# Four moved query units, a decoding laid out by ranks, and four PSUM banks for the token rows of a two-layer diffusion block

## The reference

```python
q = (xc @ wq).reshape(128, 8, 2, 128)                 # 8 heads, two half queries
s1 = einsum('thd,hnd->thn', q[:, :, 0], k1)           # scores against 128 keys, twice
s2 = einsum('thd,hnd->thn', q[:, :, 1], k2)
v1, i1 = top_k(s1, 16);  v2, i2 = top_k(s2, 16)
cand = v1[..., :, None] + v2[..., None, :]            # 16 x 16 pairs
cidx = i1[..., :, None] * 128 + i2[..., None, :]
top_s, pos = top_k(cand, 16)
eidx = take_along_axis(cidx, pos)                     # 16 experts for each head: 128 per token
g = softmax(top_s)
h = gelu(einsum('thkd,td->thk', eu[eidx], xc))        # a dot with each expert's row
y = einsum('thk,thkd->td', g * h, ev[eidx])           # weighted sum of its other row
```

## Time and profile before

| | |
|---|---|
| three runs | 2995.09, 3000.06, 3001.91 us; median 3000.06 |
| profiled execution | 2992.15 us, of which the span is 2990.3 |
| busy | PE 2379.1 us (80%), DVE 1900.5 (64%), ACT 469.3 (16%), POOL 729.8 (24%) |
| TensorE's granted clock | 0.798 of full speed on average |
| DMA | 1029.87 MB, mean 344 GB/s; the gathers are 805.36 MB of it |

### The profile page before, as it was taken

One profiled execution on the slowest core, in us unless ns is written; L12 is line 12 of the kernel. 1 busy time (PEld: TensorE's weight loads), 2 busy tenths in 40 slices (PEclk: granted clock), 3 DMA queues, 4 the chain that ended last, 5 costly groups with the idle time before them and its releaser, 6 DMA issues.

```text
span 2990.3 us, 34802 instructions
## 1 busy us (share of the span) xinstructions
PE 2379.1 (80%) x11960; PEld 1309.5 (44%) x11960; DVE 1900.5 (64%) x6178; ACT 469.3 (16%) x1139; POOL 729.8 (24%) x779
## 2 busy tenths in 40 slices
PE   7989997878999778567979988887798576665565
PEld 6868893444656445124545543332695111121111
DVE  2879987776655557857854455665458855555555
ACT  3151131233010011012010012221321010000000
POOL 0000003222222222332223223332002333333332
PEclk7999997887999889568979987675898556566557
DMA  8718858998999989879999999999445989999997
GB/s 309 273 61 318 312 213 328 388 375 332 406 384 414 414 320 369 343 319 370 373 377 420 420 403 384 404 397 373 177 148 231 367 348 418 400 381 418 402 400 287
DMA packets 155376, 1029.87 MB, mean 344 GB/s; under 512 B 19136, under 2 KB 29888, under 8 KB 34496
## 3 DMA queue, kind: packets, MB, share of 16 engines
q0 software_dynamic: 110592, 805.36, 66.8%
q1 hardware_dynamic: 31648, 209.70, 18.0%
q10 hardware_dynamic: 12960, 12.59, 1.3%
HBM read 1018.66 MB, written 8.91 MB: 344 GB/s over the span
## 4 chain that ended last, share of the span: by engine, by line
PE 52%; DVE 21%; DMA 19%; issue 3%; ACT 3%; POOL 1%; ACTq 1%; DVEq 0%; SPq 0%; POOLq 0%
DMA ring<-in_peer_uv,eT 17%; PE PS L1434 14%; DVE ring L2625 9%; PE PS L972 8%; PE PS L1453 6%; PE PS L894 4%; PE PS L999 2%; PE PS L1018 2%; PE PS L1084 2%; PE PS L896 1%; POOL ring L784 1%; PE PS L1287 1%; PE PS L1188 1%; PE PS L1061 1%; PE PS L851 1%
## 5 line engine op out<-in xcount | busy, mean ns | idle before, releaser
L2625 DVE CUSTOM_DVE_ANT_0 ring<-ring,PS 128x512 f32<-128x512 f32 x1536 | 994.1, 684 | 772.4 <-PE PS L1453 598.0
L784 POOL DMA_INDIRECT ring<-in_peer_uv,eT x768 | 728.2, 948 | 2230.1 <-PE PS L1434 1397.1
L1453 PE MATMUL PS<-xr,onesb 3*128 3x512 bf16 x1536 | 517.7, 470 | 396.3 <-DVE hcol L2625 335.8
L1434 PE MATMUL PS<-ring,zcol 128*32 128x512 f32 x3072 | 566.4, 876 | 90.1 <-DVE zcol L2635 88.3
L1453 PEld LDWEIGHTS PS<-xr,onesb 3*128 3x128 bf16 x1536 | 105.1, 95 | 920.3 <-DVE hcol L2625 496.9
L1434 PEld LDWEIGHTS PS<-ring,zcol 128*32 128x32 f32 x3072 | 102.0, 140 | 368.8 <-issue 219.6
L972 PE MATMUL PS<-uT,W 128*128 128x256 f32 x1024 | 246.4, 389 | 0.0
L1937 ACT ACTIVATE ge<-hdot 128x4 f32<-128x4 f32 x192 | 39.5, 206 | 1281.0 <-DVE hdot L2630 1281.0
L972 PEld LDWEIGHTS PS<-uT,W 128*128 128x128 f32 x1024 | 191.6, 192 | 48.2 <-issue 23.4
L2012 DVE CUSTOM_DVE_ANT_0 ring<-ring 128x1024 f32<-128x1024 f32 x160 | 190.1, 1221 | 8.1 <-DMA ring<-in_w_rows 3.9
L894 PE MATMUL PS<-uT,W 128*128 128x256 f32 (+1 forms) x672 | 154.5, 383 | 8.2 <-ACT uT L1526 7.8
(11 more groups left out here) (358 smaller groups left out, 2313.9 us busy)
## 6 DMA issues: line engine op xcount, KB each, us to landing
ring<-in_w_rows SPq DMA_DIRECT2D x40, 1024.0 KB, 8.1
W<-in_w_in SPq DMA_DIRECT2D x30, 1024.0 KB, 9.4
W<-in_w_gate SPq DMA_DIRECT2D x16, 1408.0 KB, 6.2
W<-in_w_gate SPq DMA_DIRECT2D x16, 1280.0 KB, 7.5
W<-in_w_out SPq DMA_DIRECT2D x20, 1024.0 KB, 5.0
W<-in_w_gate SPq DMA_DIRECT2D x16, 1152.0 KB, 10.5
ring<-in_w_q SPq DMA_DIRECT2D x16, 1024.0 KB, 13.5
xr<-xrows ACTq DMA_DIRECT2D x768, 6.0 KB
```

The costliest lines, as they stand in the source:

```text
L784: pool.indirect_dma_start(ring[:, slot, :], None, (peer_uv0, peer_uv1)[b.l], bass.IndirectOffsetOnAxis(eT[:, f % 2, t:t + 1], 0)).then_inc ...
L1434: last = T.matmul(PS[k * NR:(k + 1) * NR, (6 + h) * 512:(7 + h) * 512], zcol[:, g % 2, k, NR - 1 - at:2 * NR - 1 - at], ring[:, slot, D + ...
L1453: T.matmul(bank(x_bank(q, n) + h), onesb[p0:p0 + 3, 0:1].to_broadcast([3, P]), xr[p0:p0 + 3, g % 2, h * 512:(h + 1) * 512], start=True, st ...
L2625: V.tensor_tensor_reduce(out=u_half, in0=u_half, in1=bank(x_bank(q, n) + h), scale=1.0, scalar=0.0, op0=ALU.mult, op1=ALU.add, accum_out=h ...
```

## The change

1. In a latent block's end the last four query units of the second tile (`BEHIND = 4`), with the scores that need them, are formed in the first "late" steps, behind `TILE_READY`, where tokens run. The indices are turned behind unit 8 and the weights behind unit 9; the token rows are asked for behind unit 5.
2. `picked` lays its table out as place, rank, head, with the eight heads innermost, always for all heads. The reduction becomes four sums of halves. `decoded` writes the ranks with heads innermost, and `places_kept` lays out the kept indices so.
3. In the stages named in `X_BANKS` the token rows of LAT0 and CTX0 have four PSUM banks (0, 1, 4, 5), and TensorE sends the next token's broadcast along with a token's own where both fall into the same stage (`x_ahead`). The units of all fronts and the output products of the context back have two banks (2 and 3) instead of four. `x_back` waits for the dots that read a bank before a stage uses it otherwise.
4. Small constants share a tile; `iota_b` holds each number eight times.

```diff
+BEHIND = 4
+X_BANKS = {("front", "unit"): (0, 1, 4, 5), ("front", "sel"): (0, 1, 4, 5),
+           ("back", "out"): (0, 1, 4, 5)}
...
-        def x_bank(q, n):
-
-            return 2 * (n % 2) if ORDER[q] == LAT1 and n >= P else 0
+        def x_plan(stages):
+
+            banks, used = [], {}
+            for n in range(len(ORDER) * TOK):
+                own = X_BANKS.get(stages[n], (0, 1)) if n < 2 * TOK else (2, 3) if n >= 2 * TOK + P and n % 2 else (0, 1)
+                for h in range(2):
+                    b = min(own, key=lambda k: used.get(k, -1)) if len(own) > 2 else own[h]
+                    used[b] = len(banks)
+                    banks.append(b)
+            return banks
+
+        def x_ahead(stages, n):
+
+            return len(X_BANKS.get(stages[n], (0, 1))) - 2 if n + 1 < 2 * TOK and stages[n] == stages[n + 1] else 0
...
+        def unit_bank(n, c1=TOK):
+
+            return bank(2 + n % 2, 0, c1)
...
-                    if n >= 4:
-                        evacuated(n - 4)
+                    if n >= 2:
+                        evacuated(n - 2)
...
-                for u in range(16):
+                for u in range(16 - BEHIND):
                     unit(1, u)
...
-                    if u == 11:
+                    if u == 8:
                         pe.wait_ge(a["xcut"], a.at("xcut", 3))
                         pe.wait_ge(a["idx"], a.at("idx", 1))
                         T.transpose(bank(6, 0, P), isel_a[:, 0, :], ident[:, :]).then_inc(a["idxT"], 1)
-                    if u == 13:
+                    if u == 9:
                         pe.wait_ge(a["sel"], a.at("sel", 1))
                         T.transpose(bank(7, 0, P), ts[:, :, :].rearrange("p h k -> p (h k)"), ident[:, :]).then_inc(a["selT"], 1)
-                scores(1, 7)
-                pe.wait_ge(a["wo_s"], a.at("wo_s", base + 32))
                 yield TILE_READY
                 for q in range(LATE):
+                    u = 16 - BEHIND + q
+                    if u < 16:
+                        unit(1, u)
+                    if u <= 16 and u % 2 == 0:
+                        scores(1, u // 2 - 1)
                     yield "late"
...
                 r0, r1, r2 = row_banks(f, tt)
+                x_back(2, 3, 4, 5)
...
+            def x_back(*banks):
+
+                for b in banks:
+                    if x_used.get(b, -1) >= 0:
+                        pe.wait_ge(dotted, x_used[b] + 1)
+
+            def broadcast(i):
+                whole, h = i // 2, i % 2
+                q, g, k = whole // TOK, whole % TOK // GRP, whole % GRP
+                if k == 0 and h == 0:
+                    pe.wait_ge(xr_land[g % 2], 16 * (q * NG // 2 + g // 2 + 1) * GRP)
+                x_back(x_banks[i])
+                x_used[x_banks[i]] = i
+                p0 = 32 * ((k + h) % GRP)
+                T.matmul(bank(x_banks[i]), onesb[p0:p0 + 3, 0:1].to_broadcast([3, P]),
+                         xr[p0:p0 + 3, g % 2, h * 512:(h + 1) * 512], start=True, stop=True).then_inc(xb_s, 1)
...
+                        while sent[0] < 2 * whole + 2 + x_ahead(woven["pool"].stages, whole):
+                            broadcast(sent[0])
+                            sent[0] += 1
...
-                for h0 in (0, HEADS // 2):
-                    for e in range(2):
-                        picked(1, h0, HEADS // 2, e, hot_s, isel_s)
-                        yield
+                for e in range(2):
+                    picked(1, e, hot_s, isel_s)
+                    yield
...
+            def places_kept(tt):
+
+                ch.link(V.tensor_copy(i16f[:, tt, :, :, :],
+                                      i16[:, tt * SEG:(tt + 1) * SEG, :].rearrange("p (h e) k -> p e k h", e=2)))
+
+            def picked(tt, e, hot, index):
+
+                grid = [P, TOPK, TOPK, HEADS]
+                ch.link(V.tensor_tensor(hot[:, :, :, :], abf[:, e, :].rearrange("p (k h) -> p k h", h=HEADS).unsqueeze(1).to_broadcast(grid),
+                                        iota_b[:, :, :].unsqueeze(2).to_broadcast(grid), ALU.is_equal))
+                ch.link(V.tensor_tensor(hot[:, :, :, :], hot[:, :, :, :], i16f[:, tt, e, :, :].unsqueeze(2).to_broadcast(grid), ALU.mult))
+                for width in (8, 4, 2):
+                    ch.link(V.tensor_tensor(hot[:, 0:width, :, :], hot[:, 0:width, :, :], hot[:, width:2 * width, :, :], ALU.add))
+                ch.link(V.tensor_tensor(index[:, e, :].rearrange("p (h k) -> p k h", h=HEADS), hot[:, 0, :, :], hot[:, 1, :, :], ALU.add))
```

More of the change, by code:

```diff
@@ L138, in __init__ @@
         self.seen, self.ready, self.done, self.limit = [], 0, 0, TT * P
+        self.stage, self.stages = None, []
     def token(self, experts):
+        self.stages.append(self.stage)
         next(experts)
@@ L154, in run @@
                 self.seen.append(step)
+                self.stage = (what, step)
                 if step == TILE_READY:
@@ L166, in run @@
                 self.limit += P
+            self.stage = None
 class Chain:
@@ L278, in build @@
         band = sb("band", [P, TT, TOK])
-        iota_b = sb("iota_b", [P, TOPK], BF16)
-        iota = sb("iota", [P, TOPK])
-        ones = sb("ones", [P, 1])
+        iota_b = sb("iota_b", [P, TOPK, HEADS], BF16)
+        hsum = sb("hsum", [P, 2, HEADS])
+        iota = hsum[:, :, :].rearrange("p a h -> p (a h)")
+        singles = sb("singles", [P, 4])
+        ones, zero, eps = [singles[:, k:k + 1] for k in range(3)]
         onesb = sb("onesb", [P, 1], BF16)
@@ L1208, in back @@
                 begun = []
+                if s == 1:
+                    x_back(4, 5)
                 if b.early:
@@ L1244, in back @@
                         slot = arrived()
-                    if n >= 4:
-                        pe.wait_ge(a["wo_s"], a.at("wo_s", n - 3))
+                    if n >= 2:
+                        pe.wait_ge(a["wo_s"], a.at("wo_s", n - 1))
                     for k in range(KD):
-                        last = T.matmul(bank(2 + n % 4, 0, TOK), W[:, slot, k * 2 * P + n % 2 * P:k * 2 * P + (n % 2 + 1) * P],
+                        last = T.matmul(unit_bank(n), W[:, slot, k * 2 * P + n % 2 * P:k * 2 * P + (n % 2 + 1) * P],
                                         mT[:, k, :], start=(k == 0), stop=(k == KD - 1))
@@ L1444, in experts @@
                             pe.wait_ge(a["sel_s"], a.at("sel_s", 2))
-                        if k == 0:
-                            pe.wait_ge(xr_land[g % 2], 16 * (q * NG // 2 + g // 2 + 1) * GRP)
-                        for h in range(2):
-                            if whole:
-                                turns = 1 if n and x_bank(q, n) != x_bank(q, n - 1) else 0
-                                if whole > turns:
-                                    pe.wait_ge(dotted, 2 * (whole - turns) - 1 + h)
-                            p0 = 32 * ((k + h) % GRP)
-                            T.matmul(bank(x_bank(q, n) + h), onesb[p0:p0 + 3, 0:1].to_broadcast([3, P]),
-                                     xr[p0:p0 + 3, g % 2, h * 512:(h + 1) * 512], start=True, stop=True)\
-                                .then_inc(xb_s, 1)
+                        while sent[0] < 2 * whole + 2 + x_ahead(woven["pool"].stages, whole):
+                            broadcast(sent[0])
+                            sent[0] += 1
                         if k == 0 and g % NR:
@@ L1566, in front @@
                 if r in BESIDE:
-                    chosen(BESIDE[r], at_of["back", BESIDE[r]], 1, 5)
+                    chosen(BESIDE[r], at_of["back", BESIDE[r]], 1, 3)
                     yield "sel"
@@ L1721, in apart @@
                         x_rows(b.f, 1)
+                    if u == 7:
+                        exponents(a, 0)
                     if u == 8:
-                        exponents(a, 0)
-                    if u == 11:
                         act.wait_ge(a["idxT"], a.at("idxT", 1))
                         A(eT[:, b.f % 2, 0:P], bank(6, 0, P), ACT.Copy).then_inc(a["sel_s"], 1)
-                    if u == 13:
+                    if u == 9:
                         act.wait_ge(a["selT"], a.at("selT", 1))
                         A(gT[:, b.f % 2, 0:P], bank(7, 0, P), ACT.Copy).then_inc(a["sel_s"], 1)
-                scores(1, 7)
                 yield TILE_READY
                 for q in range(LATE):
+                    u = 16 - BEHIND + q
+                    if u < 16:
+                        unit(1, u)
+                    if u <= 16 and u % 2 == 0:
+                        scores(1, u // 2 - 1)
                     yield "late"
@@ L2507, in apart @@
                 bounded_pairs(a)
-                ch.link(V.tensor_copy(i16f[:, 0:SEG, :], i16[:, 0:SEG, :]))
-                decoded(0, HEADS, dec_a)
-                for h0 in (0, HEADS // 2):
-                    for e in range(2):
-                        picked(0, h0, HEADS // 2, e, hot_a, isel_a)
+                places_kept(0)
+                decoded(dec_a)
+                for e in range(2):
```

(2 more changed lines are left out.)

87 lines of the change are left out of this document (41 added, 46 removed).

## The result

Seven runs of the changed kernel gave 2977.18 to 2988.87 us, median 2983.32; seven of the kernel before 2995.09 to 3002.0, median 2996.45. The ratio is 0.9946 (0.9933 to 0.9958), some 16 us; it is worked out from all the runs, and the two medians alone lie 13 us apart. Forecast were 2980 against 3000, a ratio of 0.9933, 20 us.

What follows compares the result with a forecast made beforehand. DMA transfers were taken as 90 to 100% busy in nearly every window from the first gather on. Starts 10, late gathers -2, selections 6 and fronts 6 make 20 us off the median 3000.06: 2980 us, range 2962 to 2996 (8 in 10).

Steps and rivals of the forecast that it cites:

- The pick: VectorE's decoding of selections: one pick of all heads by ranks takes 4.35 us; two save 4.3 against picked halves.
- the rival that the decoding isn't faster: Rows of eight too short for the product's price, first token gains only 1 us per turn; 2996 us, chance 0.09.
- The starts: Start of the first and third turns: first dot 4.3 to 5.5 us earlier, credited 5 each, 10 in all.
- units 9, 10, 11 (1.79 each): Start of a turn: TensorE work left between its wait for the indices and the first broadcast, 1.79 us per unit.
- The late gathers: Behind each start: tenth gather 17 to 19 us after the first dot, charged 1 us per turn, bound 0 to 4.
- The full selections: Context turn's first tile and third turn's second tile: faster picks save 3.1 us each, 6 in all, bounds 2 and 6.
- The fronts: First and second front: less VectorE work and rows sent ahead win 2 and 4 us, bounds 0 and 14.
- the transfers' share would rise: Sign of being right: the DMA share of the second front goes above 0.94.
- The transfers absorb it: Rival: earlier starts are given back wherever a stage is bound by bytes; some 10 us gained, 2990 us, chance 0.20.
- The late units in the way: Rival: moved units at half clock delay tokens in the late steps; 14 us slower, 3014 us, chance 0.09.
- The copies hold the units back: Rival: with two banks late copies stop TensorE at 75 units and outputs; 50 us in all, 3030 us, chance 0.03.
- A third turn that isn't shorter by 6 us: Sign of being wrong: the third turn is not shorter by 6 us or more.

Runs made afterwards that it cites:

- units_kept: Changed kernel with the four query units not moved and the turns behind units 11 and 13; 2980.40 us, ratio 0.9942 to the kernel before.
- before_again: The kernel before, unchanged, profiled a second time to show the spread between single profiles; the whole differs by 3.3 us from the first profile.
- ranks_only: The kernel before with the decoding by ranks alone, units, turns and banks as before; 2989.85 us, ratio 0.9961.
- behind_only: The kernel before with the four moved units and earlier turns alone, old decoding; 3002.11 us, ratio 1.0013.
- the filled fronts: Changed kernel with 16 idle transposes ahead of the first unit of both fronts, 2981.54 us, ratio 0.9947; with turn behind unit 10 and two units moved, 2977.20, 0.9934.
- turn_10: Changed kernel with the indices turned behind unit 10 and the weights behind unit 11, four units moved; 2981.51 us, ratio 0.9929 to the kernel before.
- two_behind_again: Second measurement of the changed kernel with the turn behind unit 10 and two units moved in place of four; 2981.22 us, ratio 0.9946.
- banks_only: The kernel before with the bank plan and the broadcast sent ahead alone; 2991.77 us, ratio 0.9965.
- no_ahead: Changed kernel without the next token's broadcast sent ahead, bank plan kept; 2991.42 us, ratio 0.9977 to the kernel before.
- turn_10_two_behind: Changed kernel with the turn behind unit 10 and two units moved in place of four, first measurement; 2978.20 us, ratio 0.9920.

## Why the prediction was right, and where it was off

The measured ratio has the forecast's 0.9933 at the edge of its interval; in the range (2962 to 2996) the time lies well inside, and faster by over 0.2% had 0.77. The time is nearer than the gain: 20 us were taken off a median of 3000.06 that came down to 2996.45 with four more runs, so behind the miss of 3 us stands a gain of 16 (13 by the medians) for 20. By its own steps, with both profiles of the changed kernel, changes between tokens from the table:

**The pick** is 4.44 us for 4.35 forecast. The compare has the price of the product's row, as taken; only the last sum into f32 was low (0.374 for 0.29). The bound of 6.4 us fell, and with it the rival that the decoding isn't faster. By the Trainium skill's rule (Vector Engine (DVE) Microarchitecture Reference, section 5.1) a pick was 4.35 us; the trace agrees to 0.09, and a row of eight neighbours has the price of a row of 16.

**The starts**, forecast 5 us each: the first dot is 3.7 and 3.1 us earlier in the first turn (5.1 and 4.5 by token 8), 3.1 and 4.6 in the third; from the first compare to the first dot it is 3.5 and 2.7, 2.6 and 2.7. The term was too large by up to a half. The step that failed is "units 9, 10, 11 (1.79 each)": behind the wait that this step itself puts there units 9 and 10 ran at the lower level and took 3.41 and 2.43 us on the chain of waits, 2.3 us more. And the split was wrong in kind: I gave the earlier indices and the moved units one sum, and thought the indices alone worth about 1 us at a start. They are worth 2.2 and 1.8, the moved units add 0.5 to 1.3, and behind the start this is taken back. Removing them from the change costs nothing that can be seen, and alone they are a loss of some 4 us, 2.7 of which arise at the two starts. With the turn behind unit 10 the start has the forecast's size (6.6 and 7.1, with two units 5.1 and 5.1).

**The late gathers**: the tenth at 17.8 and 18.3 us (forecast 17 to 19), the token that needs it dotted 25.7 and 25.9 us behind the first dot (forecast some 25), in the kernel before 26.8 and 24.9. So the late gather can have cost 1 us in the third turn and nothing in the first. The changed kernel loses 1.4 us from token 8 to 24, but so do kernels without late gathers (above), and 0.9 and 0.7 from 512 to 536, where units_kept gains 0.5. The forecast of 1 each is not contradicted, and not shown.

**The full selections**, forecast 3 each: 3.0 and 3.1 us from token 230 to 256, 3.3 with the ranks alone. But 0.8 to 1.8 come there in kernels without the ranks too (before_again, the units alone, the banks alone). From 230 to 240 the ten profiles with the ranks stand at -3.2 to -3.4 and those three at -0.9 to -1.5, so the ranks' own part is 1.7 to 2.5 us, and 3.2 against the first profile. (The DMA engines were not 90% busy in every stretch, as the prediction has it from the windows of the earlier trace rows: the share before is 0.80 from 1240 to 1335 us, which is where this gain lies.) In TensorE's timeline of the changed kernel each of its two waits for VectorE's picks there is shorter by 1.5 to 1.7 us, this one against 6.46 in the earlier trace rows:

```profile
1268.37 1.21 PE L1470 MATMUL PS<-xr,onesb 3*128 3x512 bf16 x2 [4.77 <-DVE hcol L2680]
```

In the third turn it is 0.7 and 1.0 us from 536 to 556, where the kernels without the ranks stand at +1.9 to +2.3 and the first profile of before at 0: there the gain can be read as anything from 1 to 3, no more can be said from these profiles.

**The fronts**, forecast 2 and 4: 2.3 and 2.2 us in the first against the first profile and 5.0 and 4.9 against before_again, whose entry ran at the lower level too; by token 230 nothing of it is left (from 24 to 230 the changed kernel loses 1.8 and 0.8, before_again 0). 4.2 and 8.1 in the second, -3.9 to -8.2 over all that send ahead and -8.2 with the banks alone. The term was low, by up to half. I took the middle of 0 and 10 with TensorE's busy share as the reason; the row that counted was VectorE's 20.4 us of waits for broadcasts, of which a third to a half went. That the transfers' share would rise was wrong in the changed kernel's first profile (0.92) and right in its second (0.95) and with the banks alone (0.97); without the sending ahead it is 0.93.

**What I had not priced** took back what the second front gave: 4.1 and 3.0 us from token 56 to 230 and 2.3 and 1.6 from 310 to 390; KV1A's units brought 3.0 and 3.8, and 430 to 511 took 2.9 and 4.4. The first of these has no cause that I can show: all twelve profiles of altered kernels lose 1.2 to 6.9 there, ranks_only (5.1) and behind_only (4.1) among them, and before_again gains 2.7. The last is a pattern: from 430 to 511 every kernel that sends ahead gives back 2.0 to 6.0 us, and the others lose at most 1.3. What was won in KV1A is given back behind it. By what, stays open; the DMA share of that stretch is 0.94, below the 0.98 to 1.00 of the stages where I called the transfers the bound, and no run was made for it.

**The rivals.** The transfers absorb it: this may be so for the filled fronts. Its time was added up wrongly: its terms give 14 us less 2 for the late gathers, 2988 and not 2990, and against 3000 that is a ratio of 0.996, just outside the measured interval. So it is not the account of the whole, but only by a little. The late units in the way: no wait of over 0.84 us in the first late steps, and no sign of 14 us; but the moved units alone are a loss, as this rival had it. The cause is another in the main: 2.7 us of it are the longer wait and the lower level at the two starts, ahead of the first dot and not between tokens. The copies hold the units back: TensorE waits for no unit's copy in either front of the changed kernel. The Trainium skill's advice to rotate groups through several banks (Perfetto Trace Analysis, section Matmuls) is not contradicted: two banks still rotate, and a copy of 0.47 us lies under a half unit of 2.0; no wait shows that these units missed the other two banks. "A third turn that isn't shorter by 6 us" was my sign of being wrong, and it came: from token 511 to the end it is 2.0 and 3.3 us shorter, 4.4 and 5.7 against before_again. The whole came out near because the second front and KV1A, of which one was priced low and the other not at all, paid for the short starts and selections, and stretches that nobody priced took part of it back. The mechanisms were right; that their sizes summed to 16 of 20 us is partly luck.

## What to carry to other kernels

Look for the waits of a consumer on the path (here VectorE for a broadcast row of 0.4 us of TensorE work) before widening anything else: one more row sent ahead was worth 9 to 10 of the 16 us, one line on top of the four banks that it needs. When a wait is made earlier so that other work may move behind it, ask what ends next: here the fifth token's first dot stood 19 to 23 us behind the first gather in all versions, so what counted was mainly an earlier first gather. Its transfer was not what held it: the rows had landed 16.4 to 17.4 us behind the first gather in the third turn. And take a second profile of the kernel before, ahead of placing a gain of 3 us, and measure a stage from an event inside it: the first compare to the first dot agreed to 0.01 us where the tokens' times differed by 0.4.

## What was not expected of the hardware

TensorE's level behind one and the same wait is not settled by the wait. At the entry of the first front it waited 2.12 to 2.17 us in every kernel. The half unit behind it took 1.99 us (2.4 GHz) in the first profile of before, ranks_only, turn_10 and two_behind_again, and 3.4 to 3.8 (the lower level, 1.2 GHz) in before_again, the changed kernel twice, behind_only, banks_only, no_ahead, units_kept and turn_10_two_behind. Two programs stand on both sides: before, and the changed kernel with two units moved. At the second front it waited 2.18 to 2.30 us, and the same half unit took 3.66 to 3.78 in all twelve unfilled profiles. With the wait cut to 0.23 us by idle transposes it was 1.99 both times. And a gather of 1 MB that goes out into idle queues can be used 5.8 us later, not only after the 8.5 to 9 that the rows before showed, where TensorE had been the last: there too the rows had landed after 5.7 to 5.8.
